# Extra TensorE products at the waits of a two-block transformer kernel, and a new order of the latent strips

## The reference, cut to what matters

```python
def first_block(x, ...):                    # 2 layers
    for l in range(DEPTH):
        h = rms_norm(x, norm_g[l])
        q, k_c, v_c, ..., z_conv = split(h @ w_in[l])
        y_nsa = nsa_attention(...)          # compressed, selected and window branches
        y_lru = rg_lru(...)
        y_conv = conformer_conv(...)
        x = x + mixed @ w_out[l]
def second_block(x, mem, ...):              # layer 0: mixer_ab, layer 1: mixer_cd
    for i in range(DEPTH):
        x = x + mixer_ab(h, ...) if i % 2 == 0 else x + mixer_cd(h, ...)
        x = x + memory_cross_attention(...)
        x = x + swiglu(...)
def mixer_cd(h, ...):
    cq, ckv, kr, qd, kd, vd = _split(h @ w_in, CD_SIZES)
    q = (rms_norm_2(cq, g_cq) @ w_uq)       # 8 heads of 64 plain + 32 rotated columns
    q_rope = apply_rope_2(q_rope, ang_c)
    kv = (rms_norm_2(ckv, g_ckv) @ w_ukv)
    oc = blocked_dense_attention(qc, kc, v_c, ...)   # called C2 below
    od = neighbourhood_attention(qd, kd, vd, ...)    # called D2 below
    return concatenate([oc, od]) @ w_out
```

## Time and profile before

| | us |
|---|---|
| median of 3 runs | 2298.33 |
| lowest and highest | 2295.43, 2300.52 |
| the profiled execution's own time | 2302.18 |
| its span in the trace | 2300.4 |
| its mean granted TensorE clock | 0.975 of full speed |

### The profile page before, as it was taken

One profiled execution on the slowest core, in us unless ns is written; L12 is line 12 of the kernel. 1 busy time (PEld: TensorE's weight loads), 2 busy tenths in 40 slices (PEclk: granted clock), 3 DMA queues, 4 the chain that ended last, 5 costly groups with the idle time before them and its releaser, 6 DMA issues.

```text
span 2300.4 us, 33157 instructions
## 1 busy us (share of the span) xinstructions
PE 2193.3 (95%) x12066; PEld 1771.5 (77%) x12066; DVE 1246.5 (54%) x2614; ACT 1078.2 (47%) x2160; POOL 853.8 (37%) x665
## 2 busy tenths in 40 slices
PE   7999899999988999889999999999889999999997
PEld 6788667888866788668788888888657888888886
DVE  6997683499778446886552112234656555221222
ACT  6632474464247652775453223333556545332332
POOL 4433204443330343105255545544010424554553
PEclk9999799999999999999999999999989999999998
DMA  5234002332410223204233333342110323333332
GB/s 172 82 96 139 19 2 78 102 91 78 142 37 11 79 86 112 60 2 119 56 97 100 93 109 97 94 133 78 42 58 20 97 78 88 96 94 101 95 95 69
DMA packets 107184, 189.73 MB, mean 82 GB/s; under 512 B 12048, under 2 KB 22800, under 8 KB 106896
## 3 DMA queue, kind: packets, MB, share of 16 engines
q1 hardware_dynamic: 101136, 178.67, 26.6%
q10 hardware_dynamic: 5888, 8.95, 1.2%
HBM read 182.85 MB, written 2.10 MB: 80 GB/s over the span
## 4 chain that ended last, share of the span: by engine, by line
PE 84%; DVE 10%; issue 2%; ACT 2%; POOL 0%; DMA 0%; DVEq 0%; ACTq 0%
PE bank L849 23%; PE bank L851 23%; PE bank L850 23%; PE bank L1069 4%; PE bank L1082 3%; PE bank L1057 2%; DVE temp L1891 2%; DVE bank L2007 1%; PE bank L1051 1%; PE bank L1048 1%; DVE temp L1923 1%; PE bank L914 1%; DVE temp L1925 1%; PE bank L961 0%; POOL w_lo L2166 0%
## 5 line engine op out<-in xcount | busy, mean ns | idle before, releaser
L2166 POOL TENSOR_TENSOR w_lo<-w_raw,w_hi 128x512 fp32r<-128x512 f32 (+3 forms) x618 | 824.8, 1341 | 1356.2 <-ACT w_hi L1189 1355.7
L849 PE MATMUL bank<-op_hi,w_hi 128*128 128x512 f32 x1840 | 732.0, 398 | 17.8 <-DVE op_lo L1537 9.8
L851 PE MATMUL bank<-op_hi,w_lo 128*128 128x512 f32 x1840 | 718.6, 391 | 0.0
L850 PE MATMUL bank<-op_lo,w_hi 128*128 128x512 f32 x1840 | 718.3, 390 | 0.0
L1189 ACT ACTIVATE w_hi<-w_raw 128x512 fp32r<-128x512 f32 (+2 forms) x634 | 385.5, 617 | 683.5 <-PE bank L851 679.0
L849 PEld LDWEIGHTS bank<-op_hi,w_hi 128*128 128x128 f32 x1840 | 346.6, 188 | 101.1 <-issue 16.4
L850 PEld LDWEIGHTS bank<-op_lo,w_hi 128*128 128x128 f32 x1840 | 346.9, 189 | 73.7 <-issue 4.1
L851 PEld LDWEIGHTS bank<-op_hi,w_lo 128*128 128x128 f32 x1840 | 346.4, 188 | 73.3
L1607 DVE TENSOR_TENSOR temp<-bank,rstd 128x512 f32<-128x512 f32 x151 | 104.4, 692 | 400.2 <-PE bank L851 380.1
L849 PE MATMUL bank<-side_hi,w_hi 128*128 128x512 f32 (+1 forms) x628 | 234.0, 373 | 4.9 <-DVE op_lo L1689 4.3
L850 PE MATMUL bank<-side_lo,w_hi 128*128 128x512 f32 (+1 forms) x628 | 231.7, 369 | 0.0
(11 more groups left out here) (265 smaller groups left out, 2245.1 us busy)
## 6 DMA issues: line engine op xcount, KB each, us to landing
w_raw<-in_weights SPq DMA_DIRECT2D x620, 256.0 KB, 2.7
w_raw<-in_weights SPq DMA_DIRECT2D x32, 192.0 KB, 2.3
temp<-temp SPq DMA_DIRECT2D x40, 64.0 KB, 2.0
x_t<-in_x SPq DMA_DIRECT2D x8, 256.0 KB, 5.0
conv_area<-in_mem ACTq DMA_DIRECT2D x2, 1024.0 KB, 5.6
out_y<-ybuf SPq DMA_DIRECT2D x8, 256.0 KB, 2.1
conv_area<-in_bias ACTq DMA_DIRECT2D x1, 1920.0 KB, 8.7
conv_area<-in_bias ACTq DMA_DIRECT2D x2, 960.0 KB, 6.0
```

The lines of the kernel that those rows point to most:

```text
L849: pe.matmul(dst, w[0], m[0], start=start, stop=False)
L850: pe.matmul(dst, w[0], m[1], start=False, stop=False)
L851: return pe.matmul(dst, w[1], m[0], start=False, stop=stop)
L2166: pool.tensor_tensor(w_lo[:, j, 0:n], w_raw[:, p % RAW_RING, 0:n], w_hi[:, j, 0:n].bitcast(F32), ALU.subtract).then_inc(*mark("weights_spl ...
```

## The change

It has two parts. The first gives PE products whose results nobody reads: `warm(dst, count)` multiplies the identity by a 128x512 constant in plain 32 bit floats into a bank that is free there.

- Before everything, three products of the parameters with themselves, once these have landed.
- In `pe_end`, after PE has said that it is done and before it waits for ACT and DVE: 1 product before NSA, 4 before AB2, 1 before D2, 1 before C2, 2 before X2 (`WARM_END`).
- In `turn`, before the wait for the finished tile: 2 products at tile 0 of NSA, D2, C2 and X2, 1 at tile 0 of AB2, 3 at tile 30 of NSA (`WARM_TURN`). The wait for bank 4 or 5 is put ahead of the wait for the tile; both remain.
- Part AB: 1 product before its second strip, and 3 before the transposes of its second value strip.

These are 38 products: 3 at the start, 12 in NSA, 4 in AB, 5 at AB2, 8 at X2, 3 each at D2 and C2.

The second part is in C: `LATENT_ORDER` has both `uq` strips first and the strip `("qc", 1)` two places later; ACT's high half of a rotated strip moves from `side` to `late`, DVE's low half from `late` to `later`; and POOL's `rope_keys` moves from after C's strip 4 to after its last strip.

```diff
+WARM_END = {"NSA": 1, "AB2": 4, "D2": 1, "C2": 1, "X2": 2}
+WARM_TURN = {"NSA": {0: 2, 30: 3}, "AB2": {0: 1}, "D2": {0: 2}, "C2": {0: 2}, "X2": {0: 2}}
...
-LATENT_ORDER = (("uq", 0), ("qc", 0), ("uq", 1), ("qc", 1), ("kc", 0), ("vc", 0), ("qc", 2), ("kc", 1), ("vc", 1), ("qc", 3), ("kc", 2),
+LATENT_ORDER = (("uq", 0), ("uq", 1), ("qc", 0), ("kc", 0), ("vc", 0), ("qc", 1), ("qc", 2), ("kc", 1), ("vc", 1), ("qc", 3), ("kc", 2),
                 ("vc", 2), ("kc", 3), ("vc", 3))
...
@@ -850,6 +852,11 @@
+            def warm(dst, count):
+
+                for _ in range(count):
+                    pe.matmul(bank[dst][:, :], ident, C("causal"), start=True, stop=True)
+
...
@@ -927,6 +934,8 @@
+                    if s.kind == "v" and s.idx == 1:
+                        warm(7, 3)
                     pe.wait_ge(*taken(n))
...
@@ -1061,10 +1070,12 @@
                 def turn(t):
                     a = t["a"]
 
+                    if a >= 2:
+
+                        pe.wait_ge(*after("probs_copied", a - 2))
+                    warm(4 + a % 2, WARM_TURN[part[0]].get(a - ts[0]["a"], 0))
+
                     pe.wait_ge(*after("probs", a))
-                    if a >= 2:
-
-                        pe.wait_ge(*after("probs_copied", a - 2))
...
@@ -1136,13 +1147,17 @@
-            def pe_end(k):
+            def pe_end(k, part):
                 pe.drain().then_inc(*mark("part_ended_pe", ("P", k)))
+                warm(7, WARM_END[part])
                 pe.wait_ge(*after("part_ended_act", ("A", k)))
...
+            pe.wait_ge(*after("par_in", 0))
+            for _ in range(3):
+                pe.matmul(bank[7][:, :], par[:, 0:P], par[:, 0:T], start=True, stop=True)
...
+                        if step[1] == ("AB", 0) and n == rng[1]:
+                            warm(4, 1)
                         for _ in begun.pop(n, None) or strip(n, STRIPS[n].operand not in seen, between):
...
@@ -1319,7 +1336,7 @@
-                if s.kind not in ("qn", "kn"):
+                if s.kind not in ("qn", "kn", "uq"):
                     roped(n)
...
             def late(n):
                 s = STRIPS[n]
+                if s.kind == "uq":
+                    roped(n)
...
             def later(n):
+                s = STRIPS[n]
+                if s.kind == "uq":
+
+                    hi, lo = latent("rope", s.idx)
+                    dve.wait_ge(*after("roped_high", s.units[0]))
+                    settle(dve.tensor_tensor(lo, rr2[s.idx], hi.bitcast(F32), ALU.subtract))
                 if STRIPS[n].kind in ("qn", "kn"):
...
-                if s.kind == "uq":
-
-                    hi, lo = latent("rope", s.idx)
-                    dve.wait_ge(*after("roped_high", s.units[0]))
-                    settle(dve.tensor_tensor(lo, rr2[s.idx], hi.bitcast(F32), ALU.subtract))
...
@@ -2157,7 +2177,7 @@
-            keys = part_range(STRIPS, ("C", 0))[4]
+            keys = part_range(STRIPS, ("C", 0))[-1]
```

More of the change, by code:

```diff
@@ L1062, in turn @@
                     a = t["a"]
-                    pe.wait_ge(*after("probs", a))
                     if a >= 2:
                         pe.wait_ge(*after("probs_copied", a - 2))
+                    warm(4 + a % 2, WARM_TURN[part[0]].get(a - ts[0]["a"], 0))
+                    pe.wait_ge(*after("probs", a))
                     for b in range(1 if t["cmp"] else len(t["pv"])):
@@ L1144, in _ @@
             seen = set()
-            for step in PROGRAM:
+            pe.wait_ge(*after("par_in", 0))
+            for _ in range(3):
+                pe.matmul(bank[7][:, :], par[:, 0:P], par[:, 0:T], start=True, stop=True)
+            for at, step in enumerate(PROGRAM):
                 kind = step[0]
@@ L1165, in _ @@
                 elif kind == "end":
-                    pe_end(step[1])
+                    pe_end(step[1], next(later[1][0] for later in PROGRAM[at:] if later[0] == "attend"))
                 elif kind == "final":
```

## The result

The changed kernel takes 2279.07 us (median of 4 runs, 2276.59 to 2279.89), beside 2299.43 for the kernel before in the same comparison. The ratio is 0.9916, with a 95% interval from 0.9897 to 0.9934: faster by 0.8%. The forecast was 2279, its range 2266 to 2292.

The account below looks back on a forecast made before the run. TensorE was taken as the bound, with 84% of the chain and 102.4 us of stretches at half clock. Gains by place summed to 23.1 us, from the profiled 2302.18 to 2279 us; eight times in ten 2266 to 2292.

Parts of the forecast that it names:

- The clock falls after PE has waited, and PE then pays twice: Before nearly every lower-clock stretch PE idles long; it pays for the wait and the slowed work. 15 stretches, 102.4 us.
- Rival 1: The products don't hold the clock; only part C gains and two overruns are paid: 2299 us, no change, chance 0.13.
- The price of a microsecond at the lower clock: From NSA's front in both layers: 13.7 us more at the lower clock cost 5.36 us, 0.39 for each.
- NSA's front in layer 0: Products at the start of layer 0's NSA attention gain 5.0 us [-1.5 to 8.9], from layer 1 being 5.36 ahead.
- Tile 30: Three products fill PE's wait at NSA's tile 30 and prevent the fall behind it: 2.4 us for both layers [-3.8 to 3.4].
- D2: Three products, at the part's end and at tile 0, gain 1.0 us [-1.5 to 2.8].
- X2: Products at X2 in both layers gain 2.0 us [-3.4 to 3.4]; tile 0's two were about even with the wait.
- Part C's strips, 6.0: The new order and later keys shorten PE's waits and avoid a clock fall: 6.0 us, bounds 1.4 to 7.2.
- Rival 2: Part C's new order gives nothing because DVE gates the banks as before: 2285 us, chance 0.12.
- C2's front, 4.5: Products remove the 17.1 us lower-clock stretch where PE is busy throughout: 4.5 us gained [-1.5 to 8.6].
- for their tile 0 I use NSA's 1.5: At tile 0 of D2 and C2, NSA's overrun of 1.5 us was taken as the bound of the loss.
- The signs named beforehand: Lower-clock stretches of 30 to 60 us, tile 30 filled; against it, transposes following products without idle time at the lower clock.

Follow-up runs that it names:

- after_again: The changed kernel with no edit, measured again in a later comparison: median 2277.27 us, ratio 0.9925 to the kernel before.
- before_again: The kernel before with no edit, run and profiled a second time: 2296.22 us in one run.
- tiny: The changed kernel with each product behind the start only 32 of its 512 columns wide: 2285.18 us, ratio 0.9965 to the kernel before.
- order_only: The changed kernel without any of its 38 products; part C's new order and moved keys stay: 2287.35 us, ratio 0.9974 to the kernel before.
- order_no_keys: The changed kernel without products and with POOL's keys back after part C's strip 4: 2294.06 us, ratio 0.9991 to the kernel before.
- c2_one: The kernel before with a single product, at part C's end ahead of C2, and the bank wait first: 2291.04 us, ratio 0.9984.
- keys_only: The kernel before with only POOL's rotated keys moved behind part C's last weight piece: 2288.71 us, ratio 0.9992.
- more: The changed kernel with two more products at part A's fourth strip and at NSA's tile 71 in both layers: 2272.90 us, ratio 0.9908.
- more_no_start: The kernel of more without the three products before everything: 2272.41 us, ratio 0.9905 to the kernel before.

## Why the prediction was right, and where it was not

**The total** was right, and so was its remark that a usual execution has less to win. 65 executions of before in the three comparisons have a median near 2294.5; 17.2 us separate it from after_again. That 2279 is met to 0.1 us is luck. Against the first execution of before, the nine places of the sum behind the start gained 29.3 us in the profiled execution, not the 23.0 forecast. Two places that the sum has at nothing lost 3.8: tile 71 of NSA in both layers, 2.3, and the first strips, 1.6, where before_again loses as much with nothing changed. And the median of the four is 2.5 us above the profiled execution.

**The waits and the clock.** "The clock falls after PE has waited, and PE then pays twice." Shown, by `tiny` against after_again: with the same instructions and a sixteenth of the columns, 7.9 us are lost again and 68 us of stretches are back. Rival 1 falls with it. What the forecast lacks is that a wait does not fix how long the stretch behind it lasts (20.5 and 6.8 us in before and before_again).

**The price of a microsecond at the lower clock**, 0.39 us, was read from two fronts. The reading took whole stretches, 20.5 and 6.8 us, though both begin ahead of tile 0's transposes; of the time that was compared, 17.0 and 4.0 us lie in them, which makes 5.36 / 13.0 = 0.41. The 65 executions of before agree, with nothing changed between them. Their mean granted clock runs from 0.974 to 0.985 and their times from 2285.06 to 2302.05; a straight line through them has 1.78 us for each 0.001 of clock (correlation -0.97), and 0.001 of 2294 us is 4.59 us at the lower level. 1.78 / 4.59 = 0.39. The Trainium skill's page "TensorE: Matmul & The Clock Gate", section "HAM oscillation — how this bites in real kernels", takes a flat half. This kernel does not agree: even C2's front, where PE is busy throughout, pays 7.22 us for 17.1, which is 0.42.

**NSA's front in layer 0, 5.0.** A step that failed, though the total hides it. I took the difference of the two layers as what the products would win. before_again has 5.32 of it without them, so it belonged to the first execution, as the forecast suspected for the whole but not in the term. The changed kernel is 0.6 us ahead of before_again there. The overrun was 1.5 us as written (tile 0 at 252.66 against 251.21).

**Tile 30, 2.4 for two.** Measured 1.38 and 1.28 against before_again, 2.7. In layer 1 the traces of order_only, order_no_keys, c2_one and tiny met a stretch of 13.6 us, which costs 3.6 more; the two executions of before and keys_only had 3.4 there, so how often the products keep off the long one is not known. Not foreseen: where tile 30 is filled, tile 71 meets a stretch of 6.8 us, and 2.0 us go back in layer 0. This is the prediction's "the clock falls after PE has waited" at a wait that it had not looked at; `more` removes it.

**NSA's front in layer 1**, 0.5: 0.8. **AB's second strip**, 0.8: 1.1 in the profiled execution, 2.3 in after_again. **AB2**, 0.8: 1.5. **D2**, 1.0: 2.8 against before_again; but order_only has 1.9 of it without a product, so 0.9 is the products'. **X2**, 2.0: 1.5, all in layer 0, and the kernels without products have it too. I can't credit it to them. The sum also prices only the two products at tile 0; the two at the part's end have no line in it.

**The start**, 0.1: right. The third strip begins 0.37 us sooner, and more_no_start is no slower.

**Part C's strips, 6.0** [1.4 to 7.2]: 5.7. order_only, order_no_keys and keys_only show the two halves of it in their traces. Rival 2 falls.

**C2's front, 4.5** [-1.5 to 8.6]: 5.8 in the trace, near in size and wrong by cause. The step that failed is "for their tile 0 I use NSA's 1.5": C2's tile 0 waits only 0.31 us, so both products are nearly all overrun, at the full clock. One product at C2's end gains 7.22, with the two at tile 0 5.78, and 1.4 is the difference. And the product at the end is one of three edits (the others are the order and the keys' move) each of which has a trace without the long stretch. By the intervals none of the three alone gains in a usual execution what its trace shows, so 5.8 us may be more than C2's front is usually worth. These rows are of before_again and of order_only, PE's last transpose of part C and C2's first score in each:

```profile
1707.26 0.66 PE L936 MATMUL bank<-consts,conv_area 128*128 128x128 f32 x4 [0.69 <-ACT conv_area L1304]
1708.86 0.50 PE L1048 MATMUL bank<-op_hi 64*128 64x512 f32 x2 [0.94 <-DVEq L1983]
```

```profile
1702.28 0.66 PE L943 MATMUL bank<-consts,conv_area 128*128 128x128 f32 x4 [0.69 <-ACT conv_area L1315]
1703.88 0.50 PE L1055 MATMUL bank<-op_hi 64*128 64x512 f32 x2 [0.94 <-DVEq L1997]
```

The same waits, 0.69 and 0.94 us, stand in both. Behind the first the clock falls for 17.1 us, behind the second it doesn't. Why is not shown. Two readings are open. One is that the fall hangs on what PE waited earlier in part C; but keys_only keeps the 2.63 us there and is free of the stretch, with only the 1.42 us shortened, to 0.33. The other is that it hangs on the moment at which the waits come, which every edit ahead of C2 shifts; NSA's front, with the same waits and two lengths, speaks for something of this kind. No run varied either alone.

**The signs named beforehand.** Right: 34 us of stretches; none over 7; tile 30; part C's first score 5.7 us sooner; ACT's wait of 0.53. Wrong by a little: tile 0 to tile 14 takes 17.6 and 17.3 us, not 18 to 19, as tile 0 itself is late. And one of the signs against me came: at NSA's fronts the transposes follow the last product without idle time at the lower clock. At C2's tile 0 they do so too, at the full clock. It cost about what was written, 1.5 us in NSA's layer 0 and 1.4 at C2, and was won back at NSA alone.

## What to carry to other kernels

Look for waits of TensorE that a drop of the clock follows (at NSA's tiles 30 and 71 they were 3.24 and 2.15 us), and give it enough work to fill them; size it to the wait in the row of that very place, since everything over it is paid in full. Profile the unchanged kernel twice before a stretch at the lower clock goes into a sum: here 5 of 23 us were one execution's. And check a gain that a trace shows at one place against the spread of many executions, as the 7.2 us at C2's front did not come out in the medians. After filling one wait look at the next of the same length, and where a wait can be removed, as in part C, do that first.

## What was not expected of the hardware

- The kernel before takes 2285.06 to 2302.05 us (on each of the three chips its executions spread over 13 to 17 us), and 0.011 of mean granted clock goes with it. With the products the changed kernel's six executions lie within 4.8 us, at 0.988 to 0.990, and those of `more` within 2.8, at 0.993 to 0.995. Filling waits made the time steady as well as shorter.
- A stretch may cost nothing: at tile 71 that of 3.4 us in before (352.1) and none in order_only come out within 0.1 us, as PE waits for the next strip there in any case (1.55 us in order_only, 0.15 in before).
